# One product in two is summed into an open PSUM bank, some loads are issued earlier, and VectorE's list is reordered where the resident matrix changes

## What is computed

```
h      = RMSNorm(x)
proj   = h @ w_in ; gates = sigmoid(h @ w_gate + b_gate)
y0, y1, y2 = window attention, trailing-window mean pooling, attention into memory
merged = sum_i gates_i * (y_i @ w_branch_i)
x      = x + merged @ w_out
hm     = RMSNorm(x)
x      = x + relu(hm @ w_up)^2 @ w_down
out    = RMSNorm(x)
```

## Time and profile before

| | us |
|---|---|
| median of three runs | 2647.43 (2646.28 to 2653.03) |
| the profiled execution, its own time | 2650.28 |
| its span in the profile | 2648.5 |
| TensorE busy | 2576.3 (97%) |
| VectorE busy | 1859.8 (70%) |
| ScalarE busy | 1143.5 (43%) |
| GpSimd busy | 544.7 (21%) |

### The profile page before, as it was taken

How to read it: one execution, slowest core, us unless ns; L and a number is a source line. 1 busy time by engine, 2 the same in 40 slices (tenths; PEclk the granted TensorE clock), 3 DMA queues, 4 the chain that set the end, 5 groups by cost and what they waited for, 6 DMA issues and landing times.

```text
span 2648.5 us, 33224 instructions
## 1 busy us (share of the span) xinstructions
PE 2576.3 (97%) x12017; PEld 2131.1 (80%) x12017; DVE 1859.8 (70%) x2766; ACT 1143.5 (43%) x2107; POOL 544.7 (21%) x509
## 2 busy tenths in 40 slices
PE   8999999999998999998998999999999999999998
PEld 7888887888886887876887888878887888888886
DVE  8777767666566656657778677766668677686896
ACT  6344543344434433333545454555455233242433
POOL 1444200000021152234554443000000111111100
PEclk9999999999999999999999999999999999999999
DMA  5677554676446777767788666543345676767742
GB/s 172 218 258 250 187 187 159 191 237 198 146 114 232 247 243 259 228 210 267 213 253 277 227 215 195 183 149 108 109 147 173 120 208 124 176 157 157 200 175 112
DMA packets 346749, 508.71 MB, mean 192 GB/s; under 512 B 33192, under 2 KB 213468, under 8 KB 346588
## 3 DMA queue, kind: packets, MB, share of 16 engines
q1 hardware_dynamic: 318940, 431.08, 50.3%
q0 software_dynamic: 27648, 75.51, 11.8%
HBM read 325.12 MB, written 181.40 MB: 191 GB/s over the span
## 4 chain that ended last, share of the span: by engine, by line
PE 79%; DMA 7%; DVE 6%; POOL 3%; issue 3%; ACT 1%; SPq 1%; DVEq 0%; POOLq 0%; ACTq 0%
PE ps L2153 25%; PE ps L2154 25%; PE ps L2155 25%; DMA t_d<-tin 2%; DMA rows_tm<-in_x 2%; DVE s_lo L1511 1%; PE ps L2158 1%; DMA tin<-in_w_down 1%; PE ps L2395 1%; PE ps L2372 1%; DVE res_lo L1517 1%; PE ps L2341 1%; DMA tin<-in_w_out 1%; POOL tin L2057 0%; POOL tin L2059 0%
## 5 line engine op out<-in xcount | busy, mean ns | idle before, releaser
L2153 PE MATMUL ps<-res_hi,s_hi 128*128 128x512 f32 x3084 | 1206.8, 391 | 16.7 <-issue 13.8
L2154 PE MATMUL ps<-res_lo,s_hi 128*128 128x512 f32 x3084 | 1203.3, 390 | 0.0
L2155 PE MATMUL ps<-res_hi,s_lo 128*128 128x512 f32 x3084 | 1202.7, 390 | 0.0
L2153 PEld LDWEIGHTS ps<-res_hi,s_hi 128*128 128x128 f32 x3084 | 580.9, 188 | 140.3 <-issue 17.6
L2155 PEld LDWEIGHTS ps<-res_hi,s_lo 128*128 128x128 f32 x3084 | 580.9, 188 | 121.0
L2154 PEld LDWEIGHTS ps<-res_lo,s_hi 128*128 128x128 f32 x3084 | 581.1, 188 | 119.2
L1054 ACT ACTIVATE s_hi<-piece_f 128x512 fp32r<-128x512 f32 x440 | 275.7, 628 | 455.0 <-PE ps L2155 439.3
L1054 ACT ACTIVATE s_hi<-s_sum 128x512 fp32r<-128x512 f32 x327 | 204.5, 628 | 355.1 <-PE ps L2155 345.3
L1511 DVE TENSOR_TENSOR s_lo<-piece_f,s_hi 128x512 fp32r<-128x512 f32 x436 | 326.7, 750 | 28.1 <-ACT s_hi L1054 25.8
L1511 DVE TENSOR_TENSOR s_lo<-s_sum,s_hi 128x512 fp32r<-128x512 f32 x327 | 243.7, 746 | 86.7 <-ACT s_hi L1054 86.7
L1561 DVE TENSOR_TENSOR u<-u,ps 128x512 f32<-128x512 f32 x109 | 74.7, 685 | 304.5 <-PE ps L2155 304.5
(11 more groups left out here) (180 smaller groups left out, 2619.1 us busy)
## 6 DMA issues: line engine op xcount, KB each, us to landing
proj_d<-c SPq DMA_DIRECT2D x152, 256.0 KB, 3.0
piece_f<-in_w_up SPq DMA_DIRECT2D x32, 1024.0 KB, 6.9
up_d<-c SPq DMA_DIRECT2D x128, 256.0 KB, 3.0
piece_f<-up_d SPq DMA_DIRECT2D x32, 1024.0 KB, 8.3
piece_f<-in_w_gate SPq DMA_DIRECT2D x24, 1024.0 KB, 7.4
w_hi<-parts_d SPq DMA_DIRECT2D x48, 512.0 KB, 3.8
w_lo<-parts_d SPq DMA_DIRECT2D x48, 512.0 KB, 4.8
temp<-proj_d SPq DMA_DIRECT2D x48, 512.0 KB, 6.3
```

The costliest lines, as they stand in the source:

```text
L2153: mm(dst, wh, xh, start=first, stop=False)
L2154: mm(dst, wh, xl, start=False, stop=False)
L2155: return mm(dst, wl, xh, start=False, stop=last)
```

## The change

Six things change.

- A12's product is summed into A11's bank, and S4's into S1's (`ADDED_TO`). TensorE goes on in that bank once `p1` has been copied out, and once C22 has been taken from S1's bank. So a piece fills five banks in place of seven, and `acc` gives them by another rule (`bank_at`); who must have emptied a bank before TensorE opens it changes with it.
- VectorE's second `u2` (line 1563) and its C11 (line 1573) are gone. C11 is ready in PSUM: ScalarE applies tanh, or relu and square, or a plain copy straight from the bank (`finish`), and VectorE adds it to rows straight from the bank (`add_row`).
- In the first piece of a job VectorE subtracts slot seven behind C22, not ahead of it. In the last piece before a job of which one slot is loaded early it empties turned rows (`take_ht`) ahead of slot three.
- Two slots of the job of w_out are loaded while the mixers still run, and piece 39 ahead of slots four to seven.
- The last rows are normalized and stored in two halves, the half that is ready first ahead.
- Two semaphores are merged into one, and ScalarE issues one more tiny copy at the start.

```
+    OWN_BANK = {A11: 0, S2: 1, S1: 2, S3: 3, A22: 4}
+    ADDED_TO = {A12: A11, S4: S1}
+    BEFORE = {S1: U2, S3: C12, A22: U3}
+    def bank_at(n, i):
+        return (5 * n + OWN_BANK[ADDED_TO[i] if i in ADDED_TO else i]) % 6
     def acc(n, i):
-        return ps[:, (PROD * n + i) % 6, :]
+        return ps[:, bank_at(n, i), :]
...
+                    if e == (0, NBLK - 1, 3):
+                        sp.wait_ge(pv_done, 4 * NBLK)
+                        load_slot(OUT_JOB, 0)
+                        load_slot(OUT_JOB, 1)
...
             def out_fetch():
                 sp.wait_ge(mv_done, 4 * NBLK)
-                load_slot(OUT_JOB, 0)
                 load_piece(IN_END)
-                load_slot(OUT_JOB, 1)
                 load_slot(OUT_JOB, 2)
             def out_rest():
...
+                load_piece(IN_END + 1)
                 load_slot(OUT_JOB, 3)
...
                 load_slot(OUT_JOB, 6)
-                load_piece(IN_END + 1)
...
             def finish(n, which, order):
-                if not gates(n) and not squares(n):
+                if adds_rows(n) or plain(n) and which != C11:
                     return
                 tile = c_tile(n, which)
-                act.wait_ge(ev_dve, 7 * n + which)
+                taken_from = tile[:]
+                if which == C11:
+                    act.wait_ge(prod, PROD * n + A12 + 1)
+                    taken_from = ps[:, bank_at(n, A12), :]
...
+                if plain(n):
+                    op(tile[:], taken_from, ACT.Copy).then_inc(c11_rdy, 1)
+                    return
...
             def take_c22(n):
                 v.tensor_tensor(u3[:], u2[:], acc(n, S3), ALU.add).then_inc(ev_dve, 1)
...
-                v.tensor_tensor(u2[:], u2[:], acc(n, S1), ALU.add).then_inc(ev_dve, 1)
                 c_free(n, 0)
                 v.tensor_tensor(c22[:], u3[:], acc(n, S1), ALU.add).then_inc(ev_dve, 1)
...
-                v.tensor_tensor(dst, dst, c_tile(n, which)[:], ALU.add).then_inc(row_add, 1)
+                part = acc(n, A12) if which == C11 else c_tile(n, which)[:]
+                v.tensor_tensor(dst, dst, part, ALU.add).then_inc(row_add, 1)
...
-                    if first:
-                        r_low(j, 6)
...
                     take_c22(n)
+                    if first:
+                        r_low(j, 6)
...
-                    take(n, C11, A12, p1, 1)
                     add_row(n, C11, 0, 0)
...
                     add_row(n, C21, 1, 0)
+                    take_ht(n - 1, 0)
                     if last and early(j + 1) == 1:
                         r_low(j + 1, 2)
-                    take_ht(n - 1, 0)
...
+            def last_rows():
+                n, k = NQT - 1, normed(NQT - 1)
+                for i in (1, 0):
+                    dve.wait_ge(rs_sum, 4 * k + (2 if i else 4))
+                    v.scalar_tensor_tensor(out=rvar[:, i:i + 1], in0=ss4[:, i, 0:1], scalar=D * EPS, in1=ss4[:, i, 1:2],
+                                           op0=ALU.add, op1=ALU.add).then_inc(rs_var, 1)
...
-                        if i == S4:
+                        if i == A12:
                             pe.wait_ge(ev_act, n + 1)
-                        elif n:
-                            pe.wait_ge(ev_dve, 7 * (n - 1) + FREED[i + 1])
+                        elif i == S4:
+                            pe.wait_ge(ev_dve, POSTS * n + C22)
+                        elif i == A11 and n >= 2:
+                            pe.wait_ge(ev_dve, POSTS * (n - 2) + C21)
+                        elif i == S2 and n:
+                            pe.wait_ge(*c11_taken(n - 1))
+                        elif i in BEFORE and n:
+                            pe.wait_ge(ev_dve, POSTS * (n - 1) + BEFORE[i])
...
                             last = product(dst, s_hi[:, slot, k, :], s_lo[:, slot, k, :], res_hi[:, i, k, :], res_lo[:, i, k, :],
-                                           k == 0, k == 3)
+                                           k == 0 and i not in ADDED_TO, k == 3, i in ADDED_TO)
```

More of the change, by code:

```diff
@@ L568, in build @@
     S_NEED = {S1: 1, S3: 2, S2: 3, S4: 4}
-    U2, U3, U4, C22, C11, C21, C12 = range(1, 8)
-    FREED = {S2: U2, S1: C22, S3: U3, A12: C11, A22: C21, S4: C12}
+    U2, U3, C22, C21, C12, C11 = range(1, 7)
+    POSTS = 5
+    OWN_BANK = {A11: 0, S2: 1, S1: 2, S3: 3, A22: 4}
+    ADDED_TO = {A12: A11, S4: S1}
+    BEFORE = {S1: U2, S3: C12, A22: U3}
     def sums_of(n, done):
```

107 lines of the change are left out of this document (72 added, 35 removed).

## The result

The changed kernel took 2632.32 us (median of 4 runs, 2630.37 to 2636.13) beside 2646.86 of the kernel before (4 runs, 2644.64 to 2653.03): a ratio of 0.9934, 95% interval 0.9922 to 0.9947. Run again with a later batch, beside new runs of the kernel before, it gave 0.9928 (0.9914 to 0.9943; 2631.37 us against 2650.17). The forecast was 2625.0, a ratio of 0.9915: the direction and the range (2615 to 2636) hold, and the gain is 15 to 19 us instead of 22. The time lies outside the forecast case itself (2618 to 2631) and inside the stretch that was given to "transfers bind" (2631 to 2637).

A forecast was written before the change was run, and what follows sets the result against it. TensorE, busy 97%, was taken to bind, so VectorE savings pay only in its 72 us of standing still. Terms summed to 22.4 us off 2650.3, 2627.9; the median lies 2.9 lower, giving 2625.0, range 2615 to 2636.

The forecast's parts named there:

- forecast case: Whole kernel: the summed gains hold and the time falls within 2618 to 2631 us; chance 0.58.
- transfers bind: Rival: loads issued earlier meet others on the same 16 engines, land hardly earlier; gain 13 us, 2634.4; chance 0.19.
- part 1: Two VectorE additions fewer in each of 109 pieces: hidden in undisturbed pieces, value 0; S4's new wait for C22 covered.
- Part 2: Earlier slot six and seven loads at matrix changes: gains 2.7 us at piece 19, 2.5 at 62, 1.0 at 78.
- Part 3: Piece 46, turned rows ahead of slot three: rows end 2.9 us earlier; gain 2.9 us, between 1.5 and 4.
- Part 4: Loads at the mixers' end: piece 39's load some 20 us earlier, shortening piece 38's stalls; gain 8.0 us, bounds 5 and 10.
- three such overlaps cost up to 3.3: Piece 38: VectorE's work slowed beside GpSimd's three sums for piece 39, up to 3.3 us off the 9.6 us gain.
- Part 5: Inside the w_out job: 3.5 us of waits for turned rows, 0.7 less three times; gain 1.8 us (0.5 to 2.5).
- Part 6: Kernel end: scaling done 3.0 us earlier and a smaller last store; gain 4.0 us, bounds 2.9 and 4.5.
- The store's 1.0: Kernel end: the last store, 512 KB in place of 1024 KB, taken as 3.0 us where 4.0 was seen.
- Part 7: Start: S2 of piece 1 also waits for a second ScalarE copy of 0.20 us; cost 0.5 us.
- S4's wait for C22: Rival: C22 ready more than 5.4 us after S3's end makes every piece pay, about 2655 us; slower or nothing 0.04.

The follow-up runs named there:

- control: The changed kernel run again unaltered in a later batch, beside new runs of the kernel before: 2631.37 us, ratio 0.9928.
- first execution: The first profiled execution of the unaltered changed kernel, the slowest of its four runs: 2636.13 us.
- sums held: Changed kernel with GpSimd's sums for piece 39 held until VectorE has subtracted slot five of w_out: 2630.11 us, ratio 0.9919.
- slot six experiment: Changed kernel with the load of slot six issued behind the store of C21 again, at all eight matrix changes: 2638.09 us, ratio 0.9947.

## Why the prediction was right, and where it was not

- **What bounds, and that VectorE's savings pay only at stalls** (part 1's benefit): right, by the four extra additions. Part 1's value of 0 is right for undisturbed pieces only. Around the changes of the matrix one addition ahead of C22 is worth some 8 us of span in all, 3.1 at piece 19 alone. The sums of parts 2 and 4 list VectorE's work without the second `u2`, so its worth is inside terms that I had credited to the loads; how they divide was not measured.
- **Part 2**, 6.2: right in mechanism. The control gained 5.0, and taking the loads back cost 7.1. The first execution gained 3.5 since slot five landed 2 us late. At piece 62 the sum was 0.8 to 1.3 too high: A22 starts 0.2 and 0.7 us later behind A11 than the sum has it, and S4 follows 4.1 us behind A22 where the sum has 3.5.
- **Part 3**, 2.9: this step failed. The piece did gain 2.2 to 2.6, but not by the order: 2.6 with the rows behind slot three as well. I had written that VectorE's list is gapless there and decides, and then credited 2.2 us to a reordering within it. S4 needs slot seven, the last of that list; only work that leaves the list ahead of it counts. One addition put back ahead of C22 costs 0.3 us in this piece; what C11's addition is worth there was not measured alone. That the number came out is luck.
- **Part 4**, 8.0: the step that failed most. Every term of its sum lies in piece 38, and that piece gained 1.9 and 2.3. The 2.9 us at the mixers' end, which the forecast does not name, hide it in the total. Right in the mechanism: ScalarE's 11.97 us of waiting are gone, and the early load is worth 4.0. S4 bound by slot seven shows only with the sums held (1.29 us of waiting); in the changed kernel S4 of piece 38 has no gap, since the stall at S3 has made all behind it late. Mis-sized was the term "three such overlaps cost up to 3.3", which I let slot six hide: a single split beside two of the sums cost 2.9 us, and ahead of slot four, where nothing hides it. The stall then is 5.8 us and takes the clock with it: A12 starts 5.3 us behind S3 in place of 2.7. The starting point was a little high too, since S4 of piece 38 began at 1246.25 before, not at 1247.1. The Trainium skill, page "SBUF — State Buffer", section "Who interferes with whom", has the later of the two operations fully blocked. The trace agrees that one of them is shut out as a whole (3.6 us for a split of 0.68 beside 2.5 us of additions), but it was VectorE's, whose record starts first, at 1224.9 against 1225.43, and it was shut out through both additions. The total by that rule, 2627, was the nearer one.
- **Part 5**, 1.8: too small by 2.4. All three gaps inside the job went, 3.3 us, not half of them (the other 0.2 of my 3.5 lay in piece 47, and grew to 1.2). VectorE's wait for the row load fell as well, from 3.04 to 1.47 us in piece 41 and from 2.82 to 0.30 in 42. I had counted 0.7 us a piece as if each piece stood alone. One addition more ahead of C22 costs nothing in these pieces (4.15 us gained with it and without), and neither does piece 39's late load, so by elimination it is C11's addition that counts here. Argued, not tried: the load of the next rows waits for the transposes, these for VectorE, so what is saved comes back each time.
- **Part 6**, 4.0: 2.5, under my lower bound. From the last addition to the last scaling's end 2.6 us went instead of 3.0; the second power took 1.53 us beside the first scaling, and the second scaling waited 0.45 for it. (The four terms that I listed behind the last addition sum to 4.2 us, not to the 3.5 of the forecast, which needs the power hidden behind the first scaling; 3.9 were measured.) The store's 1.0 did not come in the span (-0.1), though the store landed in 2.6 us in place of 4.0. The path was wrong there: it ran on to the store alone, and GpSimd's drain behind the last power ends later.
- **Part 7**, -0.5: -0.14 and -0.35.
- **The rivals.** "Transfers bind" came nearest in time (2634.4) and fell by the slot six experiment. S4's wait for C22 costs nothing in undisturbed pieces up to 2.9 us of extra work; the price that the forecast asks 109 pieces for is paid only around the changes of the matrix.

Against the control the terms miss by -5.7 (part 4), +2.9 (the mixers' end, which no part names), +2.4 (part 5), -1.5 (part 6) and -1.2 (part 2), the small ones left out. That the total came within 3 us of that execution's gain, and 6 to 7 us of the two medians, is in good part luck: over and under cancel. What the runs add is that the change's gain lies in fewer additions and earlier loads. Of its new orders, rows ahead of slot three is worth nothing, and slot seven behind C22 is worth something only where slot seven comes late.

## What to carry to other kernels

Where one engine's list has no gap up to the operation that releases the next engine, moving work within the list changes nothing; take work out of it, or behind that operation. Where the list has a wait, what stands behind it matters: put work that is ready ahead of it. Before giving a load an earlier start, look at what else it sets going: here it started GpSimd additions that cost the critical engine more than they take. A gain worked out from one trace at a place where a transfer lands last has a scatter of its own, here 2 us at each of two places; look at a second execution before explaining it. At the end of a program look at what each engine still does behind its last operation, and not only at the last store.
